# The last two output tiles of a hybrid layer: every token block by rows, none by columns, and a prompt block last

## The reference

```python
y = jnp.einsum('btd,de->bte', merged, w_out)        # 576 x 2048 times 2048 x 2048
x_out = x + rmsnorm(y, g_post)                       # mean of y*y over all 2048 columns of a row
```

## Time and profile before

| | |
|---|---|
| time of three runs | 2236.39, 2234.29, 2235.7 us; median 2235.7 us |
| the profiled execution | 2234.09 us, of which the span of its instructions is 2232.0 us |
| PE busy | 2215.4 us, 99% of the span |
| DVE, ACT, POOL busy | 1543.4, 944.6, 179.4 us |
| chain that ended last | PE 98%, DMA 1%, DVE 1% |

### The profile page before, as it was taken

One profiled execution on the slowest core, in us unless ns is written; L12 is line 12 of the kernel. 1 busy time (PEld: TensorE's weight loads), 2 busy tenths in 40 slices (PEclk: granted clock), 3 DMA queues, 4 the chain that ended last, 5 costly groups with the idle time before them and its releaser, 6 DMA issues.

```text
span 2232.0 us, 39594 instructions
## 1 busy us (share of the span) xinstructions
PE 2215.4 (99%) x16274; PEld 2170.9 (97%) x16274; DVE 1543.4 (69%) x1787; ACT 944.6 (42%) x1274; POOL 179.4 (8%) x238
## 2 busy tenths in 40 slices
PE   8999999999999999999999999999999999999998
PEld 7999999999999999999999999999988999999998
DVE  7876767657666666767666666666678577768675
ACT  6343433334433344444444444444555234234443
POOL 0000000000100000111000000000112112100000
PEclk9999999999999999999999999999999999999999
DMA  6443453534444444444444444444765765763547
GB/s 181 116 132 106 119 142 96 156 100 125 120 126 116 127 116 116 127 116 127 119 124 116 126 117 125 118 123 131 268 220 173 256 191 176 188 172 86 137 131 261
DMA packets 420311, 319.30 MB, mean 143 GB/s; under 512 B 11677, under 2 KB 379685, under 8 KB 418736
## 3 DMA queue, kind: packets, MB, share of 16 engines
q1 hardware_dynamic: 399680, 251.18, 41.0%
q0 software_dynamic: 20224, 65.18, 8.6%
q10 hardware_dynamic: 240, 0.52, 0.1%
HBM read 254.00 MB, written 62.83 MB: 142 GB/s over the span
## 4 chain that ended last, share of the span: by engine, by line
PE 98%; DMA 1%; DVE 1%; ACT 0%; issue 0%; DVEq 0%; SPq 0%; ACTq 0%
PE pp L988 66%; PE pp L1214 13%; PE pp L1402 7%; PE M L1006 2%; PE pp L998 1%; PE M L1318 1%; PE M L1339 1%; PE M L1238 1%; PE pp L1499 1%; PE M L1175 1%; PE M L998 1%; PE M L1267 1%; PE M L1378 1%; DMA gt_lo<-gated_scratch 1%; PE pp L1485 0%; PE M L988 0%
## 5 line engine op out<-in xcount | busy, mean ns | idle before, releaser
L988 PE MATMUL pp<-xa,wa_hi 128*128 128x288 f32 x7392 | 1480.3, 296 | 0.1
L988 PEld LDWEIGHTS pp<-xa,wa_hi 128*128 128x128 f32 x7392 | 1185.5, 188 | 1.1 <-DVE zs L2144 0.4
L988 PE MATMUL pp<-xa,wa_lo 128*128 128x288 f32 x3696 | 1086.7, 294 | 0.0
L988 PEld LDWEIGHTS pp<-xa,wa_lo 128*128 128x128 f32 x3696 | 696.2, 188 | 0.0
L2034 DVE TENSOR_TENSOR wa_lo<-raw_a,wa_hi 128x1024 fp32r<-128x1024 f32 x262 | 325.9, 1247 | 238.7 <-ACT wa_hi L1521 238.6
L1521 ACT ACTIVATE wa_hi<-raw_a 128x1024 fp32r<-128x1024 f32 x262 | 276.6, 1056 | 202.7 <-PE pp L988 201.6
L2034 DVE TENSOR_TENSOR wa_lo<-raw_r,wa_hi 128x1024 fp32r<-128x1024 f32 x134 | 170.7, 1274 | 140.1 <-ACT wa_hi L1521 140.1
L1521 ACT ACTIVATE wa_hi<-raw_r 128x1024 fp32r<-128x1024 f32 x134 | 141.4, 1055 | 133.2 <-PE pp L988 125.9
L1214 PE MATMUL pp<-gt_hi,wb_hi 128*128 128x288 f32 x768 | 168.9, 302 | 0.4 <-DMA gt_lo<-gated_scratch 0.4
L1214 PE MATMUL pp<-gt_hi,wb_lo 128*128 128x288 f32 x768 | 164.5, 296 | 0.0
L1214 PE MATMUL pp<-gt_lo,wb_hi 128*128 128x288 f32 x768 | 164.1, 295 | 0.0
(11 more groups left out here) (374 smaller groups left out, 2576.4 us busy)
## 6 DMA issues: line engine op xcount, KB each, us to landing
raw_a<-in_w_in_dram SPq DMA_DIRECT2D x202, 512.0 KB, 5.0
raw_r<-in_w_in_dram SPq DMA_DIRECT2D x68, 512.0 KB, 5.0
z_scratch<-zs POOLq DMA_DIRECT2D x60, 576.0 KB, 3.3
raw_b<-in_w_branch_dram SPq DMA_DIRECT2D x48, 512.0 KB, 4.9
gz<-z_scratch SPq DMA_DIRECT2D x48, 288.0 KB, 5.2
raw_a<-in_w_out_dram SPq DMA_DIRECT2D x20, 512.0 KB, 6.4
qkv<-z_scratch SPq DMA_DIRECT2D x22, 288.0 KB, 5.3
gt_hi<-gated_scratch SPq DMA_DIRECT2D x4, 1152.0 KB, 7.4
```

The source lines that it names most:

```text
L988: i = nc.tensor.matmul(out, ws[:, slot, k, :], xa[:, o, part, k, :], start=opens and k == 0 and s == 0, stop=k == HK - 1 and s == 2, skip_ ...
```

## The change

Blocks 0 and 1 are made by rows like the other three. There is one routine for all five blocks, in the order 0, 1, 4, 2, 3. What only the columns needed goes: the two copies to `yT`, four transposes, the small scalings and squares. The reloads of the spilled tiles follow the new order. Block 1 is stored in one piece instead of two, and the sample rows in one instead of three, since block 4 is no longer last.

```diff
-Y_PART0, Y_PART0_W = (0, 1), P + 64
-Y_WHOLE = (2, 3, 4)
+Y_WHOLE = (0, 1, 4, 2, 3)
-Y_STORES = [(0, 0, D), (1, 0, D // 2), (1, D // 2, D // 2), (2, 0, D), (3, 0, D // 2), (3, D // 2, D // 2),
-            (4, 0, D // 2), (4, D // 2, D // 4), (4, 3 * D // 4, D // 4)]
+Y_STORES = [(0, 0, D), (1, 0, D), (4, 0, D), (2, 0, D // 2), (2, D // 2, D // 2),
+            (3, 0, D // 2), (3, D // 2, D // 4), (3, 3 * D // 4, D // 4)]
         def whole_bank(n):
-            return pp[:, (3, 1, 2)[n], 0:2 * P]
+            return pp[0:Y_BLOCKS[Y_WHOLE[n]][1], (3, 1, 2, 3, 1)[n], 0:2 * P]
...
             sp.wait_ge(y_reloaded, 32)
-            reload(Y_WHOLE[:-1], 0, OUT_PAIRS - 1)
+            sp.wait_ge(wb_lo_ready, H_OUT + 4)
+            reload((4,), 0, OUT_PAIRS - 1)
             sp.wait_ge(y_reloaded, 48)
-            sp.wait_ge(wb_lo_ready, H_OUT + 4)
-            reload(Y_WHOLE[-1:], 0, OUT_PAIRS - 1)
+            reload((2, 3), 0, OUT_PAIRS - 1)
...
-            def part_of_tile(v, hook_at, hook):
-                tile, part = last_step(v)
-                if v == Y_FULL:
-                    pe.wait_ge(c12_done, PAIRS + OUT_PAIRS)
-                elif v == Y_FULL + 1:
-                    pe.wait_ge(c21_done, PAIRS + OUT_PAIRS)
-                for c in range(KD):
-                    k, n = (c + HK) % KD, 2 * (tile - Y_FULL) + c // HK
-                    if v == Y_FULL and c == HK:
-                        last_product()
-                        pe.wait_ge(mlo_ready, A21_READY)
-                    if c % HK == 0:
-                        pe.wait_ge(wb_lo_ready, H_OUT + n + 1)
...
+            def whole_block(n):
+                (t0, rows), out = Y_BLOCKS[Y_WHOLE[n]], whole_bank(n).rearrange("p (t d) -> p t d", d=P)
+                if n == 0:
+                    pe.wait_ge(c11_done, PAIRS + OUT_PAIRS)
+                elif n == 2:
                     pe.wait_ge(c12_done, PAIRS + OUT_PAIRS)
+                elif n > 2:
+                    pe.wait_ge(yg_ready, Y_FULL + n - 2)
                 for c in range(KD):
                     k, half = (c + HK) % KD, c // HK
                     at = (k % HK) * P
+                    if n == 0 and c % HK == 0:
+                        if c == HK:
+                            last_product()
+                            pe.wait_ge(mlo_ready, A21_READY)
+                        pe.wait_ge(wb_lo_ready, H_OUT + 3 + half)
+                    if n == 1 and c == HK // 2:
+                        to_tokens(OUT_PAIRS - 1)
...
+            for n in range(len(Y_WHOLE)):
+                whole_block(n)
```

More of the change, by code:

```diff
@@ L960, in _ @@
             sp.wait_ge(t_ready, 4 * (PAIRS + OUT_PAIRS))
-            reload(Y_PART0, 0, OUT_PAIRS - 2)
-            reload(Y_PART0, OUT_PAIRS - 2, OUT_PAIRS - 1)
+            reload((0, 1), 0, OUT_PAIRS - 2)
+            reload((0, 1), OUT_PAIRS - 2, OUT_PAIRS - 1)
             sp.wait_ge(y_reloaded, 32)
-            reload(Y_WHOLE[:-1], 0, OUT_PAIRS - 1)
+            sp.wait_ge(wb_lo_ready, H_OUT + 4)
+            reload((4,), 0, OUT_PAIRS - 1)
             sp.wait_ge(y_reloaded, 48)
-            sp.wait_ge(wb_lo_ready, H_OUT + 4)
-            reload(Y_WHOLE[-1:], 0, OUT_PAIRS - 1)
+            reload((2, 3), 0, OUT_PAIRS - 1)
             for j, (m, c, w) in enumerate(Y_STORES):
@@ L1495, in whole_block @@
                     at = (k % HK) * P
-                    if c == hook_at:
-                        hook()
+                    if n == 0 and c % HK == 0:
[5 more added lines that the diff above has]
+                        to_tokens(OUT_PAIRS - 1)
                     for q, (xs_, ws) in enumerate(((m_hi, oc_hi_pair), (merged_lo, oc_hi_pair), (m_hi, oc_lo_pair))):
-                        i = nc.tensor.matmul(out, xs_[:, k, t0:t0 + P], ws[half][:, :, at:at + P],
+                        i = nc.tensor.matmul(out, xs_[:, k, t0:t0 + rows], ws[half][:, :, at:at + P],
                                              start=c == 0 and q == 0, stop=c == KD - 1 and q == 2)
                 i.then_inc(wb_used, 2)
[L1503 to L1511, removed]
+            for n in range(len(Y_WHOLE)):
+                whole_block(n)
         @block.scalar
@@ L1990, in _ @@
             squares(Y_FULL - 1)
[L1992 to L2000, removed]
@@ L2014, in _ @@
[L2014 to L2017, removed]
-                whole_squares(n)
[L2019 to L2025, removed]
+            def whole_squares(n):
+                m = Y_WHOLE[n]
+                rows, at = Y_BLOCKS[m][1], (640, 1664)[n % 2]
+                act.wait_ge(wb_used, whole_done(n))
+                if n >= 2:
+                    act.wait_ge(ysq_done, Y_FULL + n - 1)
+                nc.scalar.activation(M[0:rows, at:at + 2 * P], whole_bank(n), ACT.Square,
+                                     accum_out=ysums[0:rows, m, Y_FULL:Y_FULL + 1]).then_inc(ysq_done, 1)
@@ new lines, in root, with store_sample @@
+            def root(n):
+                m = Y_WHOLE[n]
+                act.wait_ge(ms_ready, n + 1)
+                nc.scalar.activation(rs_y[:, m:m + 1], ss_y[:, m:m + 1], ACT.Sqrt).then_inc(root_x_ready, 1)
+            def store_sample(j):
+                m, c, w = Y_STORES[j]
+                at, rows = Y_BLOCKS[m]
+                act.wait_ge(yout_ready, j + 1)
+                act.dma_start(y_sample[0, :, c:c + w], y_tok[TP - at:rows, m, c:c + w]).then_inc(y_stored, 16)
+            for n in range(len(Y_WHOLE)):
+                whole_squares(n)
+                root(n)
+                if n == 3:
+                    store_sample(2)
@@ L2840, in _ @@
             last_lo(3)
[L2841 to L2857, removed]
@@ L2859, in mean_squares @@
-            def mean_squares(n, a, b, tiles):
-                dve.wait_ge(ysq_done, KD + n)
+            def mean_squares(n):
+                m = Y_WHOLE[n]
+                dve.wait_ge(ysq_done, Y_FULL + n + 1)
                 steps.begin(0, 1)
-                steps.link(nc.vector.tensor_reduce(ss_y[:, a:b], ysums[:, a:b, 0:tiles], AXX, ALU.add))
-                nc.vector.tensor_scalar(ss_y[:, a:b], ss_y[:, a:b], 1.0 / D, EPS, ALU.mult, ALU.add).then_inc(ms_ready, 1)
+                steps.link(nc.vector.tensor_reduce(ss_y[:, m:m + 1], ysums[:, m:m + 1, 0:Y_FULL + 1], AXX, ALU.add))
+                nc.vector.tensor_scalar(ss_y[:, m:m + 1], ss_y[:, m:m + 1], 1.0 / D, EPS, ALU.mult, ALU.add).then_inc(ms_ready, 1)
@@ L2864, in mean_squares, with whole_scaled, inverse_root @@
                 steps.end(1)
-            def inverse_root(n, a, b):
+            def whole_scaled(n):
+                m = Y_WHOLE[n]
+                rows = Y_BLOCKS[m][1]
+                mean_squares(n)
+                nc.vector.tensor_tensor(y_tok[0:rows, m, Y_FULL * P:D], whole_bank(n), gpost_last[0:rows, :], ALU.mult
+                                        ).then_inc(yg_ready, 1)
+            def inverse_root(n):
+                m = Y_WHOLE[n]
                 dve.wait_ge(root_x_ready, NB + n + 1)
@@ L2868, in inverse_root @@
                 steps.begin(0, 1)
-                steps.link(nc.vector.reciprocal(rs_y[:, a:b], rs_y[:, a:b]))
+                steps.link(nc.vector.reciprocal(rs_y[:, m:m + 1], rs_y[:, m:m + 1]))
                 steps.end(1)
-            def whole_scaled(n):
-                mean_squares(n + 1, Y_WHOLE[n], Y_WHOLE[n] + 1, Y_FULL + 1)
-                nc.vector.tensor_tensor(y_tok[:, Y_WHOLE[n], Y_FULL * P:D], whole_bank(n), gpost_last[:, :], ALU.mult)
             def finish(j):
@@ L2881, in finish @@
                                                x_again[m][0:rows, c:c + w], ALU.mult, ALU.add).then_inc(yout_ready, 1)
-            read_part(Y_FULL)
             scale_y(Y_FULL - 2)
             scale_y(Y_FULL - 1)
-            read_part(Y_FULL + 1)
-            scale_part(Y_FULL)
-            scale_part(Y_FULL + 1)
-            mean_squares(0, 0, 2, KD)
-            inverse_root(0, 0, 2)
-            dve.wait_ge(x_again_loaded, 16 * 3)
-            dve.wait_ge(y_reloaded, 32)
-            finish(0)
-            whole_scaled(0)
-            finish(1)
-            inverse_root(1, 2, 3)
-            finish(2)
-            dve.wait_ge(y_reloaded, 48)
-            finish(3)
-            whole_scaled(1)
-            inverse_root(2, 3, 4)
-            dve.wait_ge(x_again_loaded, 16 * (NB + 1))
-            finish(4)
-            finish(5)
-            dve.wait_ge(y_reloaded, 64)
-            whole_scaled(2)
-            inverse_root(3, 4, 5)
-            for j in range(6, len(Y_STORES)):
-                finish(j)
+            dve.wait_ge(gain_y_loaded, 16 * (OUT_PAIRS + 2))
+            for n, (first, last) in enumerate(((0, 1), (1, 2), (2, 3), (3, 5), (5, 8))):
+                whole_scaled(n)
+                inverse_root(n)
+                if n == 0:
+                    dve.wait_ge(x_again_loaded, 16 * 3)
+                    dve.wait_ge(y_reloaded, 32)
+                elif n == 2:
+                    dve.wait_ge(x_again_loaded, 16 * (NB + 1))
```

(5 more changed lines are left out.)

37 lines of the change are left out of this document (2 added, 35 removed).

## The result

| | median | lowest to highest |
|---|---|---|
| before, 7 runs | 2235.7 us | 2234.17 to 2240.39 |
| changed, 7 runs | 2242.64 us | 2242.22 to 2244.68 |

The ratio of changed to before is 1.0035, 95% interval 1.0025 to 1.0045, so the change makes the kernel slower by 5.6 to 10.1 us. The profiled execution of the changed kernel took 2242.64 us, the one of before 2234.09 us. The forecast of 2242.5 us lies 0.1 us under the median. That closeness is luck: the profile shows errors that cancel in part, and the rest is made up by a high median of before. Measured again on another chip, the same pair took 2242.48 and 2234.1 us, 8.4 apart where the forecast had 6.8.

A forecast was written before the change was run, and what follows sets the result against it. PE, busy 99% of the span, was taken as the bound. Matmuls +0.85, transposes −0.44, two waits +6.7 and last stores −0.3 gave +6.8 us on the 2235.7 median: 2242.5 us, range 2240.4 to 2244.6.

The forecast's parts named there:

- a hole filled by a granted clock of 0.50 behind it: Sign that would show the forecast wrong: in PE's timeline, the clock at 0.50 (1.2 GHz) behind a wait.
- first rival: Clock falls while PE waits for weight pieces: 1.7 us lost, time 2244.2 us, chance 7%.
- The first hole: Start of the last tiles: PE waits for weight piece 2's low part from DVE, 3.69 us, 3.8 with handover.
- The four transposes: Removed from PE's stream in the changed blocks: −0.44 us.
- the narrower streaming: Blocks 0 and 1: 96 matmuls streaming 192 tokens become 96 streaming 256 columns, 0.009 us more each, +0.85 us.
- my bounds of 0.107 and 0.120: Block 1's 48 matmuls with 64 stationary columns: 0.107 to 0.120 us each; 0.120 taken, the lower takes 0.6 us off.
- The reloads were not late: Reloads before the last blocks' finishes: cost taken as 0; rival that they land late, 2245.0 us, chance 5%.
- A wait of 3.8 us is shorter than this, and the second of 2.9 shorter still: Argument against a clock fall: PE's waits are shorter than the some 5 us before the fall at the kernel's end.
- The second hole: Behind the last product: PE waits for weight piece 3's low part, 2.82 us, 2.9 with handover.
- refilling the pipeline: After each of PE's two waits: 0.1 us added for handover and refilling an empty pipeline, an estimate.
- the tail: Behind the last matmul: last stores no longer leave on ACT's slower queue, −0.3 us, between +0.3 and −0.8.
- SP moves the same bytes: Last stores: ACT has none now and SP carries the same bytes; step behind the −0.3 us.

The follow-up runs named there:

- The waits alone: Kernel before with tile 14's two waits asking for 3 and 4 weight pieces instead of 1 and 2; 2244.91 us, ratio 1.0043.
- the last product first: Changed kernel with the last product ahead of block 0, and DVE making its result and low parts 1 and 2 earlier; 2233.53 us.
- the one of 8.2: Kernel before with the row blocks in the order 4, 2, 3 instead of 2, 3, 4, measured a second time; 2235.06 us, ratio 1.0005.

## Why the prediction was right, and where it was not

The time and the main cost, the two holes, came out as forecast. By its own list of what would show it wrong, though, one sign was met: "a hole filled by a granted clock of 0.50 behind it". What happened is the two holes of the forecast and its first rival, the fall of the clock, together; PE's busy time, which should have stayed or fallen, grew. The last matmul ended 10.5 us later than before and 7.4 us followed, where 7.1 and 8.7 were expected.

**Right, by its own steps.** The first hole was put at 3.69 us and measured 3.68, the second at 2.82 and measured 2.80; both were read from the times at which DVE made pieces that nobody had waited for before. The waits alone bring the loss, and their cover given back takes it away (the last product first). The four transposes and the narrower streaming came out as summed. Block 1, with 64 stationary columns, takes 0.114 us a matmul, between my bounds of 0.107 and 0.120, 0.3 us less than the value taken. The lower bound was misread: from 256 to 288 columns the rows grow by 0.0142 us and not 0.0133, and 256 / 32 x 0.0142 is 0.114, which is what it measured. The reloads were not late: the large one was issued at 2214.50, landed 7.6 us later at 2222.1, and was wanted at 2229. The sum was in the right direction and in the range.

**Mis-sized: the clock.** I gave its fall 7%, and it fell, twice; that the forecast of the time held all the same is no merit of this step. The step that failed is "A wait of 3.8 us is shorter than this, and the second of 2.9 shorter still". I had taken one silence of 5 us at the kernel's end, for the silence that it takes. But from PE's stop to the fall it was 5.1 us there, 4.1 us at the first hole of the changed kernel (2190.83 to about 2194.95), 2.9 at the second (2202.3 to about 2205.2), and 2.3 at its end (2233.56 to about 2235.9). Nor has PE to be idle for all of that time: in most profiles it had gone back to work before the fall. One such row bounds nothing from below. The Trainium skill, page "TensorE: Matmul & The Clock Gate", section "Why this matters for your kernels", had warned of gaps of about the length of the first hole; the trace agrees with it against me at 3.68 us. The second hole, 2.80 us, is a little shorter than the gaps that the page warns of, and the clock fell there too. The price of a fall, taken from the slow transposes at the kernel's start, was 1.7 us; it measured 1.5 in this kernel, but twice. The term missing in the sum is +2.9 us for the clock and +0.4 for refilling the pipeline, of which 0.2 was in it.

**Mis-sized: the tail.** Put at −0.3, between +0.3 and −0.8, measured −1.5. The step that failed is that "SP moves the same bytes": the bytes are the same, but in three issues instead of six, and ACT's late third issue, was only the visible part: with the sample block last the tail was 8.8 to 9.2 us in every profile, whichever queue issued, and with it earlier 7.4 to 7.6, but for the one of 8.2.

**What cancelled.** Of the 8.5 us in the profile, +6.8 were forecast; missing are the clock with +2.9 us, 0.2 of refilling, block 1's −0.3 and the tail's −1.2, which make 8.4. So these errors leave 1.6 us uncovered. That the medians differ by 6.9 and not by 8.5 is due to the median of before on the first chip, 1.6 us over its profiled execution, whose 7 runs had two at 2238 and 2240 us. On the chip of the repeat the difference of medians is 8.4. The forecast built on that high median, and so its nearness is luck.

## What to carry to other kernels

When an edit reorders work, read the number in each wait and ask of the trace when that count was reached before, even where nobody waited for it: two of these times gave the two holes to 0.02 us. Price a hole on TensorE with its clock: at holes of 2.8 and 3.7 us, 1.5 us or more came on top each time. And count the issues, not only the bytes, that stand behind the last matmul.

## What was not expected of the hardware

At the lower clock, matmuls with 128 stationary columns started 0.213 us apart, whether 192 or 256 columns streamed; at full clock 0.111 and 0.120. So the one with 192 is not bound by its streaming at either clock, and the floor under it nearly doubles when the clock halves. The Trainium skill, same page, section "LDWEIGHTS (loading the stationary operand)", has a load take P / 1.2 ns for P stationary columns; that makes 107 ns for 128, an estimate from the page's formula, near the 0.111 us here. The row at the lower clock, 0.213 us, shows twice that.

The fall did not come in the middle of a hole but about at its end: over the profiles with holes, from 0.4 us before TensorE resumed to 1.3 us after. So nearly all of what the clock costs is on the matmuls behind a hole, and looks like busy time.
